# Two transformer blocks in float32 on one core: the opening of the first block projects six column pairs instead of four with unsplit weights, and the rwkv chain of layer zero has three fewer empty steps

## The reference

```
mod = silu(c) @ w_ada[l] + b_ada[l]           # six vectors of 1024: shift, scale, gate, twice
h = rms_norm(x, norm_mix[l]) * (1 + sc1) + sh1
p = h @ w_in[l]                               # qkv | rwkv (14 tiles of 128 columns) | gmlp u, v | three gates
y_rwkv = rwkv7_time_mix(p[rwkv columns])      # token shift, decay, keys, a recurrence over tokens, group norm
y_gmlp = chunked_spatial_gating(p[u, v])      # gelu, layer norm of v, a mix over tokens
merged = sum(gates * (y @ w_branch))          # three branches, then w_out and the feed-forward part
```

## Time and profile before

| | us |
|---|---|
| median of 3 runs | 2117.92 (2117.28 to 2118.41) |
| profiled execution: time | 2117.53 |
| profiled execution: span of the trace | 2115.6 |
| TensorE busy in the span | 2092.3 (99%) |
| VectorE busy | 1640.2 (78%) |
| ScalarE busy | 1234.4 (58%) |
| granted TensorE clock, mean | 1.0 |

### The profile page before, as it was taken

How to read it: one execution, slowest core, us unless ns; L and a number is a source line. 1 busy time by engine, 2 the same in 40 slices (tenths; PEclk the granted TensorE clock), 3 DMA queues, 4 the chain that set the end, 5 groups by cost and what they waited for, 6 DMA issues and landing times.

```text
span 2115.6 us, 39171 instructions
## 1 busy us (share of the span) xinstructions
PE 2092.3 (99%) x16342; PEld 1901.6 (90%) x16342; DVE 1640.2 (78%) x2520; ACT 1234.4 (58%) x2007; POOL 13.1 (1%) x20
## 2 busy tenths in 40 slices
PE   8999999999999999999999999999999999999999
PEld 7898999999998899998888989888898888998888
DVE  7899788888887788877887656787688765778876
ACT  4754755555756656555665447566475644766554
POOL 0000000000000000000000000000000000000000
PEclk9999999999999999999999999999999999999999
DMA  9566567768644467655555654555555557456553
GB/s 372 198 208 216 177 214 251 248 225 292 222 159 169 162 213 236 210 187 188 185 192 188 228 160 156 199 189 190 189 180 190 190 198 219 140 170 208 190 190 130
DMA packets 122115, 424.57 MB, mean 201 GB/s; under 512 B 13466, under 2 KB 22042, under 8 KB 121171
## 3 DMA queue, kind: packets, MB, share of 16 engines
q1 hardware_dynamic: 121938, 422.08, 59.0%
HBM read 417.68 MB, written 4.35 MB: 199 GB/s over the span
## 4 chain that ended last, share of the span: by engine, by line
PE 88%; ACT 4%; DVE 4%; DMA 2%; issue 1%; SPq 0%; POOL 0%; ACTq 0%; DVEq 0%
PE bank L208 88%; ACT arena L259 2%; DVE arena L214 2%; ACT hi L259 1%; DVE lo L214 1%; DMA raw<-W 1%; PE bank L211 1%; ACT L259 1%; DVE arena L222 1%; DMA arena<-conv_rows 0%; DVE ada L231 0%; ACT L251 0%; DVE m L214 0%; DMA xT<-x 0%; SPq L205 0%
## 5 line engine op out<-in xcount | busy, mean ns | idle before, releaser
L208 PE MATMUL bank<-h,hi 128*128 128x256 f32 (+1 forms) x5248 | 1183.0, 312 | 0.0
L259 ACT ACTIVATE hi<-raw 128x1024 fp32r<-128x1024 f32 x656 | 688.5, 1056 | 536.4 <-PE bank L208 467.0
L208 PE MATMUL bank<-h,lo 128*128 128x256 f32 x3328 | 949.0, 285 | 1.2 <-ACT arena L259 0.9
L208 PEld LDWEIGHTS bank<-h,hi 128*128 128x128 f32 x5248 | 861.4, 190 | 60.4 <-issue 1.9
L214 DVE TENSOR_TENSOR lo<-raw,hi 128x1024 fp32r<-128x1024 f32 x656 | 792.4, 1221 | 99.4 <-ACT hi L259 98.4
L208 PEld LDWEIGHTS bank<-h,lo 128*128 128x128 f32 x3328 | 633.7, 190 | 11.6 <-issue 6.9
L208 PE MATMUL bank<-act,hi 128*128 128x512 f32 x1056 | 370.0, 393 | 0.0
L208 PE MATMUL bank<-act,lo 128*128 128x256 f32 x1056 | 294.7, 279 | 0.0
L208 PEld LDWEIGHTS bank<-act,hi 128*128 128x128 f32 x1056 | 197.9, 187 | 47.3
L208 PEld LDWEIGHTS bank<-act,lo 128*128 128x128 f32 x1056 | 197.9, 187 | 0.0
L259 ACT ACTIVATE arena<-arena 128x256 f32<-128x256 f32 (+4 forms) x202 | 98.6, 493 | 158.9 <-DVE arena L214 151.4
(11 more groups left out here) (152 smaller groups left out, 1942.0 us busy)
## 6 DMA issues: line engine op xcount, KB each, us to landing
raw<-W SPq DMA_DIRECT2D x664, 512.0 KB, 4.0
ada<-WA SPq DMA_DIRECT2D x80, 512.0 KB, 3.9
arena<-WA SPq DMA_DIRECT2D x16, 512.0 KB, 14.3
arena<-conv_rows SPq DMA_DIRECT2D x16, 280.0 KB, 6.2
arena<-taps SPq DMA_DIRECT2D x2, 1792.0 KB, 8.2
p_projected<-arena SPq DMA_DIRECT2D x2, 1024.0 KB, 8.5
arena<-p_projected SPq DMA_DIRECT2D x2, 1024.0 KB, 4.8
arena<-scr SPq DMA_DIRECT2D x10, 128.0 KB, 5.0
```

The lines of the kernel that those rows point to most:

```text
L208: return self.done(lambda e: e.matmul(out, l, r, start=start, stop=stop, skip_group_check=True))
L259: return self.done(lambda e: e.activation(out, in_, f, scale=scale, **kw))
```

## The change

`PLAIN` becomes 12: pairs 1 and 4 join the plain pairs (96 tiles in 12 blocks, 12 tiles per k), in banks 0, 1, 4, 5, 7, 6. SP issues the first weight blocks in another pattern, and starts to load into buffers already used while the last w_ada blocks are still to be issued (`FIRST_TICKS`). For layer 0, `rwkv_steps` loses one "next" after square and two after bonus. In both layers "branch0" 3 moves ahead of "branch1" 0. The other edits follow from these: the counts of tiles in the starts, and gmlp v's bank (3 instead of 1 in layer 0).

```diff
-PLAIN = 8
+PLAIN = 12
 def rwkv_steps(l):
-    s = [("mix",), ("square",), "next", "next", ("lora", 0), ("lora", 1), "next", ("length",), "next", ("decay",), ("gate",),
+    s = [("mix",), ("square",), "next"] + ["next"] * l + [("lora", 0), ("lora", 1), "next", ("length",), "next", ("decay",), ("gate",),
          "next", ("scan", 0), "next", ("scan", 1), "next", ("middle",), "next", ("powers",), "next", ("until", ("z", l, 5)), ("keys",), "next",
          ("rate",), ("tok", "V", 0), "next", ("scale",), ("tok", "V", 1), "next", ("receive",), ("tok", "B", 0), "next",
-         ("bonus",), ("tok", "K", 0), "next", "next", "next", ("until", ("ln", l)), ("bonus sum",), "next", ("flag", ("prep", l))]
+         ("bonus",), ("tok", "K", 0), "next"] + ["next", "next"] * l + [("until", ("ln", l)), ("bonus sum",), "next", ("flag", ("prep", l))]
...
         s += [("branch0", l, 0), ("branch0", l, 1), ("branch0", l, 2), ("finish", ("rwkv", l)), ("pause if", (l, 4))]
-        s += [("branch1", l, 0), ("pause if", (l, 4)), ("branch0", l, 3), ("merge", l, 0), ("branch0", l, 4), ("branch1", l, 1), ("branch0", l, 5),
+        s += [("branch0", l, 3), ("pause if", (l, 4)), ("branch1", l, 0), ("merge", l, 0), ("branch0", l, 4), ("branch1", l, 1), ("branch0", l, 5),
...
-Z_START, Z_NEXT = (0, 1, 4, 5), {1: (3,), 4: (1,)}
-Z_PAIRS = ((6, 2, 3, 0), (6, 2))
+Z_START = (0, 1, 4, 5, 7, 6)
+Z_PAIRS = ((6, 2, 3, 0, 1, 4), (6, 2))
+FIRST_LOADS = ((0, 1), (2,), (3, 4), (5,), (6,), (), (), ())
+FIRST_TICKS = (0, 0, 0, 0, 1, 1, 2, 1)
...
-                        pair(MAIN if l else Z_NEXT.get(p, MAIN), item, "w_in", l, ...
+                        pair(MAIN, item, "w_in", l, ...
-                    token_rows((MAIN if q[0] else Z_NEXT[1], ONE), ...
+                    token_rows((MAIN if q[0] else STAT, ONE), ...
-                f.tiles(48)
+                f.tiles(8 * (PLAIN - 2))
...
             s.dma(par[:, 0:PAR0], T["par"][:, 0:PAR0]).then_inc(d_par0, "par0")
+            f.pause = True
             for k in range(KD):
                 load_start(k)
-                if k < RAW:
-                    load(k)
+                for b in FIRST_LOADS[k]:
+                    load(b)
+                f.tiles(8 * FIRST_TICKS[k])
...
                 elif what == "start":
-                    f.tiles(32)
+                    f.tiles(8 * (PLAIN - 4 - sum(FIRST_TICKS)))
```

More of the change, by code:

```diff
@@ L1139, in tensor_program @@
                     if p not in Z_PAIRS[l]:
-                        pair(MAIN if l else Z_NEXT.get(p, MAIN), item, "w_in", l, [("c", I_RWKV + (2 * p + j) * 128) for j in range(2)], h_in(("n1", l)))
+                        pair(MAIN, item, "w_in", l, [("c", I_RWKV + (2 * p + j) * 128) for j in range(2)], h_in(("n1", l)))
                 elif what == "rwkv":
@@ L1147, in tensor_program @@
                 elif what == "gmlp v":
-                    token_rows((MAIN if q[0] else Z_NEXT[1], ONE), [(what, q[0], c) for c in range(2)], "w_in", q[0], I_GMLP + 512, h_in(("n1", q[0])), 4)
+                    token_rows((MAIN if q[0] else STAT, ONE), [(what, q[0], c) for c in range(2)], "w_in", q[0], I_GMLP + 512, h_in(("n1", q[0])), 4)
                 elif what == "token norm":
@@ L2660, in pool_program @@
                 elif what == "start":
-                    f.tiles(64)
+                    f.tiles(8 * PLAIN)
                 elif what == "start1":
```

## The result

| us | before | after |
|---|---|---|
| median (4 runs of each, side by side) | 2117.68 (2117.28 to 2118.41) | 2134.18 (2131.95 to 2135.23) |
| profiled execution: time, span | 2117.53, 2115.6 | 2131.95, 2130.1 |
| granted TensorE clock, mean | 1.0 | 0.997 |

The ratio is 1.0076, 95% interval 1.0064 to 1.0088. That is outside the predicted range (2114 to 2126): the forecast gave +4.0 us, the profiled executions differ by 14.4 and their spans by 14.5. The profiled execution of the changed kernel is the fastest of its four, so the views explain 14.5 us of the 16.5 between the medians.

What follows compares the result with a forecast made beforehand. TensorE, busy 99%, was taken as the bound. The terms +1.8 - 1.7 - 0.9 - 1.1 + 4.5 + 2.3 - 0.9 gave +4.0 us on 2117.53, so 2121.5 us; range 2114 to 2126.

Steps and rivals of the forecast that it cites:

- 32 tiles plain, +1.8: TensorE's opening: 32 tiles plain take 13.9 us instead of 12.0 split, +1.8 us, bounds +1.5 and +2.7.
- The upper bound: For the 32 plain tiles in the opening: +2.7 us, taking 0.36 us for a split tile.
- SP's order, zero: Opening loads: last scaled k near 45 us, asked for at 51.8; up to +1 us if the queue stalls.
- Length, -1.7, and gmlp u, -0.9: Layer 0 on TensorE: the waits before the length matmuls and in gmlp u go, -1.7 and -0.9 us.
- Keys to B0: ScalarE and VectorE in layer 0: five table loads, token norm before rate; rate done at 103.5 us, TensorE asks at 99.0.
- TensorE waits 4.5 us instead of 1.07: At the turn of B0 (line 211), TensorE waits 4.5 us for VectorE, bounds 1.5 and 6 us.
- Bonus sum, +2.3: After B0's turn: TensorE arrives at 112.4 us, VectorE's bonus ends at 114.7; +2.3 us, bounds 0 and 4.
- y1l, -0.9: Before branch1 in layer 0: 12 more tiles ahead of it remove TensorE's y1l wait, -0.9 us.
- Rival B: First cross: VectorE's backlog meets modulation columns, TensorE waits at cross and levels; +7 to +10, near 2126 us; chance 0.07.
- The rule on table switches: ScalarE's table loads: 1.28 us each without drain; by the page's 1380 ns drain, two extra loads cost 2.8 us more.

Runs made afterwards that it cites:

- the bias table moved: The changed kernel with the bias table's matmul behind gmlp v instead of ahead of it: 2131.56 us, ratio 1.0068.
- the run with attention later: The changed kernel with layer 0's attention chains (scores, and max to out) one tick later: 2127.86 us, ratio 1.0047.
- SP's old order: The changed kernel with SP's old order of first loads, none into used buffers until the last w_ada block is issued: 2134.69 us, ratio 1.0078.
- closer steps: The kernel before (eight plain blocks) with layer 0's three empty rwkv steps removed, all else as before: 2122.72 us, ratio 1.0023.

## Why the prediction was wrong

The mechanism that it named as deciding, VectorE late for B0, is what happened. But the wait was priced without the clock behind it, and the sum ended before the second large wait; the bias table's wait and layer 1's opening were not in it either.

- *32 tiles plain, +1.8.* Measured +3.1. The 192 loads took 44.29 us from 14.15: 0.231 each and not 0.217. The rate per tile was right for the steady part. The other 1.3 us is the start, 0.48 us later, and 0.85 us because the first loads ran at half rate for longer in this execution (last section). In the seven other runs with twelve plain blocks they took 42.7 to 43.9 us, so this is scatter and no price of the plain tiles. The upper bound was a slip: 13.9 us less 32 tiles at 0.36 us is +2.4 and not +2.7.
- *SP's order, zero.* Right: with the old order the time is the same, and TensorE waits for no weights in the opening.
- *Length, -1.7, and gmlp u, -0.9.* Both right. Missed was the bias table's matmul, two instructions behind lora that need a bank which ScalarE empties after lora. Before, split blocks lay between; now nothing does, +1.45.
- *Keys to B0.* Five table loads between 84.8 and 97.1 us, the token norm's four ahead of rate's two: as walked. The walk was short by 3.9 us at its end (107.4 for 103.5). 1.3 of it is the later plain end and 1.5 the bias table, which hit TensorE's request as well (101.7 for 99.0). By this reckoning the other 1.1 us is ScalarE's, whose token norm activations released VectorE at 102.3 and not at 98.5; this is what raises the wait from 4.5 to 5.8, inside the bounds of 1.5 to 6. The shares are not sure: with the bias table moved, VectorE's end came only 0.6 us earlier against the plain blocks' end, and not 1.5.
- *The first step that failed:* "TensorE waits 4.5 us instead of 1.07", counted as its length. A wait this long was also the start of about 5 us at half clock, +2.4 us. The kernel before has no wait over 1.71 us in layer 0 behind its plain blocks, and full clock there, so no row gave the price and no bound was set for it. One place hinted at it and was not read so: TensorE's first matmuls run at half rate (last section).
- *Bonus sum, +2.3.* Bonus was ready at 118.6 and asked for at 118.7: no wait, since the slow TensorE came 2 us later itself. In three runs where TensorE came at full speed the wait was there, 2.3 to 3.7 us.
- *The second step that failed, and the larger one: after the first cross, nothing.* The sum ended too early. Moving the chain by one block against the stream was costed only at its own end (y1l, -0.9, right) and not against attention's chain, with which it shares VectorE and the banks: +4.2 us at step x behind attention's scores, wait and clock. Rival B had this kind of thing, a backlog that meets later work, and the prediction gave it 0.07 and 2126 us; it placed the meeting at cross and modulation, where none was.
- *The rule on table switches.* By the Trainium skill, page "ScalarE: Activation LUTs", section "What ACT_TABLE_LOAD costs", each switch also drains 1380 ns. Here an activation on 128x1024 ends at 88.12 by its row and the load starts at 88.15; the next activation starts 0.01 us behind the load (89.44). Five loads, no drain seen: the trace disagrees with the page. Two activations in a row overlap by 0.12 us (86.09 and 87.06), which a load between them prevents, so the price here is 1.28 us and this little more.

**Left open:** layer 1's opening, where TensorE's wait grew from 0.27 to 1.36 us (2.2 in the run with attention later); ScalarE there waits for a weight transfer (4.3 us at 548.5, before 2.9 at 533.9), and why it comes later was not tried. Also whether the bias table's place is worth anything by itself.

## What to carry to other kernels

A move that takes work off ScalarE and VectorE at the price of a later start of their chain is to be costed by the start: walk every product of the chain to the point where TensorE asks for it, and go on past the place of the change until the chain ends, looking at each tick for the other chains of the same engine. A wait of 2.3 us or more on TensorE, which is otherwise 99% busy here, cost its length and, in these runs, left the clock at half for another 2.9 to 6.7 us, in which half of TensorE's time is lost where its matmuls follow the clock. Where a profile shows one wait of 1.7 us and 3.4 us in hand further on, moving one empty step is the cheaper edit.

## What was not expected of the hardware

- **The clock behind a wait.** Behind all 17 waits of 2.3 us or more that TensorE has after its first 20 us, in the traces of the 13 kernels here, the granted clock was 0.50 to 0.67 over the next 3.5 us, though TensorE was busy. Behind the eleven waits of 1.25 to 1.71 us it stayed at 1.00. In between it went either way: 1.89 us had 0.63 behind it (SP's old order) and 1.92 us had 0.70 (closer steps), but 2.02 and 2.21 us had 1.00. Filling the 5.8 us wait with matmuls kept the clock at 1.00.
- **The first plain matmuls.** They run at half rate although the clock column reads 1.00. Windows of TensorE's matmuls on `raw` alone (us, busy and count, clock, DMA, GB/s), first the kernel before, then the changed one:

```profile
13.70:17.70 4.00, 4.00 (x10) 1.00 1.02 410
17.70:21.70 4.00, 4.00 (x19) 1.00 1.03 410
```

```profile
14.20:20.20 6.00, 6.00 (x14) 1.00 1.02 410
20.20:26.20 6.00, 6.00 (x29) 1.00 1.03 410
```

Ten matmuls in 4 us and then 19; in the changed kernel 14 in 6 us and then 29. A plain matmul of the kernel before takes 379 ns at the median and 767 ns at most, the ratio of the two clock levels. The start's wait of 2.9 us is not what made them slow, as TensorE was slow ahead of it already. In the kernel before this pair of 128x256 matmuls took 0.79 and 0.63 us, like the slow plain ones of the same size, where the fast ones take 0.38:

```profile
9.56 1.22 PE L208 MATMUL bank<-arena,cst 128*128 128x256 f32 x2 [0.21 <-DVE arena L214]
```

That it is the clock, the packed trace shows. It holds the granted clock as records, the first of which begins at 18.04 us in the kernel before and at 20.22 in the changed one, where the rate doubles; ahead of it there is none, and the column counts that as 1.00. If TensorE has half speed until the first record, the 192 plain loads should take their time at full speed and half of the stretch from their start to that record. In the eight runs with twelve plain blocks this stretch is 2.9 to 6.1 us and the loads take 42.72 to 44.29 us; less half of the stretch, all eight come to 41.26 or 41.27 us. The same sum gives 27.44 us for the 128 loads before, so the four added blocks cost 13.8 us at full speed, as predicted.
